# Moving 24 vector blocks of a streaming-trunk kernel from matmul bursts to row sums on VectorE

## What is computed

```python
def modulate(h, shift, scale):
    return h * (1 + scale[:, None, :]) + shift[:, None, :]
...
def sq_relu_mlp(h, w1, w2):
    return jnp.square(jax.nn.relu(h @ w1)) @ w2
```

## Time and profile before

| what | value |
|---|---|
| timed runs (us) | 3221.82, 3226.70, 3227.95; median 3226.7 |
| span of the profiled execution (us) | 3222.3 |
| time of the profiled execution beside its span | not given; span is 4.4 us (0.14%) under the runs' median |
| TensorE matmuls busy | 3134.8 us, 97% of the span |
| VectorE busy | 2185.9 us, 68% |
| ScalarE busy | 1409.6 us, 44% |
| GpSimd busy | 129.3 us, 4% |
| chain that ended last | TensorE 90%, DMA 3%, VectorE 3%, ScalarE 1% |
| moved by DMA | 669.48 MB, 208 GB/s on average |

### The profile page before, as it was taken

How to read it: one execution, slowest core, us unless ns; L and a number is a source line. 1 busy time by engine, 2 the same in 40 slices (tenths; PEclk the granted TensorE clock), 3 DMA queues, 4 the chain that set the end, 5 groups by cost and what they waited for, 6 DMA issues and landing times.

```text
span 3222.3 us, 80509 instructions
## 1 busy us (share of the span) xinstructions
PE 3134.8 (97%) x31624; PEld 2952.1 (92%) x31624; DVE 2185.9 (68%) x3943; ACT 1409.6 (44%) x2323; POOL 129.3 (4%) x245
## 2 busy tenths in 40 slices
PE   7999999998999999999999999999999999999998
PEld 3798888787999999999999988998999999999998
DVE  3676677776578978788788865455589954445445
ACT  2433436665354443333344654334464543343442
POOL 0000001110000000000000000000000000000000
PEclk9999999999999999999999999999999999999999
DMA  9887750002878888888777532432557754444443
GB/s 395 330 292 264 284 206 20 25 24 101 332 288 290 305 299 301 313 298 309 265 240 253 183 119 93 144 124 92 175 191 240 243 170 166 165 163 163 163 164 120
DMA packets 183225, 669.48 MB, mean 208 GB/s; under 512 B 21398, under 2 KB 21568, under 8 KB 182496
## 3 DMA queue, kind: packets, MB, share of 16 engines
q1 hardware_dynamic: 156096, 570.95, 49.3%
q0 software_dynamic: 26912, 95.47, 9.0%
HBM read 662.25 MB, written 4.09 MB: 207 GB/s over the span
## 4 chain that ended last, share of the span: by engine, by line
PE 90%; DMA 3%; DVE 3%; issue 1%; ACT 1%; SPq 1%; DVEq 0%; ACTq 0%; POOLq 0%
PE ps L2281 51%; PE ps L2264 8%; PE ps L2266 7%; PE ps L2265 7%; PE ps L2450 5%; DMA sb_raw<-stream 3%; PE ps L2226 1%; PE ps L2442 1%; PE ps L2215 1%; PE ps L2780 1%; PE ps L2781 1%; PE ps L2782 1%; PE ps L2824 1%; PE ps L2823 1%; PE ps L2394 1%
## 5 line engine op out<-in xcount | busy, mean ns | idle before, releaser
L764 ACT ACTIVATE sb_whi<-sb_raw 128x1024 fp32r<-128x1024 f32 x778 | 812.5, 1058 | 1124.8 <-PE ps L2281 703.8
L1252 DVE TENSOR_TENSOR sb_wlo<-sb_raw,sb_whi 128x1024 fp32r<-128x1024 f32 x778 | 942.7, 1223 | 410.8 <-ACT sb_whi L764 407.7
L2281 PE MATMUL ps<-sb_ah,sb_whi 128*128 128x288 f32 (+1 forms) x2776 | 487.0, 297 | 11.9 <-DVE sb_al L1601 8.2
L2281 PE MATMUL ps<-sb_al,sb_whi 128*128 128x288 f32 (+1 forms) x2776 | 484.4, 297 | 0.0
L2281 PE MATMUL ps<-sb_ah,sb_wlo 128*128 128x288 f32 (+1 forms) x2776 | 482.6, 296 | 0.0
L2281 PEld LDWEIGHTS ps<-sb_ah,sb_whi 128*128 128x128 f32 x2776 | 409.9, 189 | 16.9 <-issue 12.1
L2281 PEld LDWEIGHTS ps<-sb_al,sb_whi 128*128 128x128 f32 x2776 | 409.1, 189 | 0.0
L2281 PEld LDWEIGHTS ps<-sb_ah,sb_wlo 128*128 128x128 f32 x2776 | 408.6, 189 | 0.0
L2264 PE MATMUL ps<-sb_ah,sb_whi 128*128 128x288 f32 (+1 forms) x952 | 286.6, 301 | 2.0 <-DVE sb_x L1451 1.0
L2266 PE MATMUL ps<-sb_al,sb_whi 128*128 128x288 f32 (+1 forms) x952 | 283.1, 297 | 0.0
L2265 PE MATMUL ps<-sb_ah,sb_wlo 128*128 128x288 f32 (+1 forms) x952 | 282.5, 297 | 0.0
(11 more groups left out here) (350 smaller groups left out, 4665.0 us busy)
## 6 DMA issues: line engine op xcount, KB each, us to landing
sb_raw<-stream SPq DMA_DIRECT2D x1070, 512.0 KB, 4.6
sb_strip<-strips POOLq DMA_DIRECT2D x156, 512.0 KB, 5.3
sb_crow<-crow POOLq DMA_DIRECT2D x8, 512.0 KB, 5.9
sb_x<-xT SPq DMA_DIRECT2D x1, 2304.0 KB, 15.5
sb_x<-xT POOLq DMA_DIRECT2D x1, 2304.0 KB, 11.9
yT<-sb_x SPq DMA_DIRECT2D x4, 576.0 KB, 2.8
sb_lwa<-lw POOLq DMA_DIRECT2D x16, 130.0 KB, 2.5
sb_lwg<-lw POOLq DMA_DIRECT2D x16, 130.0 KB, 2.4
```

The source lines that it names most:

```text
L764: nc.scalar.activation(whi[:, q % SPL, :], raw[:, n, :], ACT.Copy).then_inc(hi_ready, 1)
L1252: nc.vector.tensor_tensor(wlo[:, q % SPL, :], raw[:, n, :], whi[:, q % SPL, :], ALU.subtract).then_inc(lo_ready, 1)
L2281: ins = mm(PS[:, m, 0:s.wide], w[:, n % SPL, a:a + P], z[:, 2 * p + j, 0:s.wide], start=False, stop=False)
```

## The change: what it does

The bursts end with m1_0_1: `HALF_GROUPS` goes from 23 to 11. The 12 bursts that go are those of m2_0_1, m1_0_2 and m2_0_2 (four each), with 48 slots of the stream, the copies to `arow` and the finishes. The strips beside m1_0 and m2_0 stay the same in number and now sum blocks 12 x 2 = 24 earlier in the list of vectors; the 24 blocks that come last before the final gate (8 of the shift and all 16 of the scale of `N_MLP1`) become *late rows*.

A late row is 32 outputs: 256 KB of weights in a layout of 128 partitions x 512 (`by_32`), loaded by GpSimd's queue into one of two buffers `late_w`, and two scalar_tensor_tensor instructions of 128x512 with an accumulator on VectorE (`late_rows`). There are 96. GpSimd issues the next load into a buffer when both instructions on it have run. GpSimd's loop over them stands ahead of the four `crow` loads and the late strips, so these now queue behind it, and the late strips also wait for all late rows.

Where the rows run on VectorE: in each of the six `beside` rounds 8 (one before `maxima`, two between `maxima` and `normalise`, one after the split behind it, two after out_lo(0), two after out_lo(1)); in each of the two closings 8 (four after the splits 4 to 7 and before out_lo(0), two after out_lo(0), two after out_lo(1)); in wo0's groups 1 to 3 and in wo1's group 1 8 each, spread by `STRIP_PLACES`. `join_late` (16 copies, 4 additions) turns the sums into `mod` at the start of wo1's group 3, ahead of `gains`.

Two loads of silu's input (`late_c`), two sigmoids on ScalarE at wdq's last slot and two multiplications on VectorE behind wdq make silu(c) in the rows' layout. `osm` and `lroot` get other places in memory, and counts that other waits use move by what was added.

```diff
-        st.append(Stage(f"m1_0_{c}", 4, 8, mixed=c < 3, epi="relu2", src="A"))
-        st.append(Stage(f"m2_0_{c}", 4, 8, mixed=c < 3, epi="resid", src="B", gate=5))
+        st.append(Stage(f"m1_0_{c}", 4, 8, mixed=c < 2, epi="relu2", src="A"))
+        st.append(Stage(f"m2_0_{c}", 4, 8, mixed=c < 1, epi="resid", src="B", gate=5))
...
-HALF_GROUPS = 6 * 4 - 1
+HALF_GROUPS = 3 * 4 - 1
...
+LATE_ROW_BLOCKS = 24
+LATE_ROWS = 4 * LATE_ROW_BLOCKS
+LATE0 = LATE_ROWS0 + LATE_ROW_BLOCKS
+ATT_ROWS, WO_ROWS, HALF_ROWS = 8, 24, 56
...
+            pool.wait_ge(silu_ready, 9)
+            for k in range(2):
+                pool.dma_start(late_w[k][:], d["late"][k]).then_inc(strip_in[k], 16)
+            with pool.Fori(1, LATE_ROWS // 2) as i:
+                for k in range(2):
+                    pool.wait_ge(strip_used, i * 4 + (LATE_USED + 2 * k - 2))
+                    pool.dma_start(late_w[k][:], d["late"][bass.ds(i * 2 + k, 1)].rearrange("a p c -> (a p) c")
+                                   ).then_inc(strip_in[k], 16)
             for i in range(4):
...
+            pool.wait_ge(strip_used, LATE_USED + 2 * LATE_ROWS)
             for k in range(2):
                 pool.dma_start(strip[:, k, :], d["strips"][STRIPS + k]).then_inc(strip_in[k], 16)
...
+                if p == 7:
+                    act.wait_ge(x_back, 128)
+                    for z in range(2):
+                        nc.scalar.activation(late_w[z][:], late_c[z][:], ACT.Sigmoid).then_inc(c_sig, 1)
...
+            def late_rows(first, n, dump, it=0, per=0):
+
+                for i in range(first, first + n):
+                    dve.wait_ge(strip_in[i % 2], it * 8 * per + 16 * (STRIPS // 2 + i // 2 + 1))
+                    if not isinstance(it, int) or i:
+                        dve.wait_ge(strip_used, it * 2 * per + (LATE_USED + 2 * i - 1))
+                    for z in range(2):
+                        nc.vector.scalar_tensor_tensor(
+                            out=late_w[i % 2][:] if z else dump, in0=late_w[i % 2][:], scalar=1.0, in1=late_c[z][:],
+                            op0=ALU.mult, op1=ALU.mult,
+                            accum_out=flat(late_sums[:, bass.ds(it * per + i, 1), z:z + 1])).then_inc(strip_used, 1)
...
+            def join_late():
+
+                dve.wait_ge(strip_used, LATE_USED + 2 * LATE_ROWS)
...
+                    if name == "wo0":
+                        late_rows(WO_ROWS + sum(STRIP_PLACES[:i]), STRIP_PLACES[i], late_scratch, it, 8)
+                    if name == "wo1" and it == 1:
+                        late_rows(HALF_ROWS + WO_ROWS + 8 + sum(STRIP_PLACES[:i]), STRIP_PLACES[i], late_dump)
...
+                            if name == "wo1":
+                                join_late()
                             gains(UNSCALED[name])
...
+            dve.wait_ge(c_sig, 9)
+            for z in range(2):
+                nc.vector.tensor_tensor(late_c[z][:], late_c[z][:], late_w[z][:], ALU.mult).then_inc(silu_ready, 1)
...
-            def outputs(it, v1, v4):
+            def outputs(it, v1, v4, rows=0):
...
                 for h in range(3):
                     out_lo(h).then_inc(S["al_done"], 1)
+                    if h < 2:
+                        late_rows(rows + 2 * h, 2, late_scratch)
...
+                rows = g0 // 4 * HALF_ROWS + it * ATT_ROWS
                 for j in (2, 3):
                     split(s, first + j)
+                late_rows(rows, 1, late_scratch)
                 maxima(v1)
+                late_rows(rows + 1, 2, late_scratch)
                 normalise(v1)
                 split(s, first + 4)
-                outputs(it, v1, v4)
+                late_rows(rows + 3, 1, late_scratch)
+                outputs(it, v1, v4, rows + 4)
...
                     for j in (4, 5, 6, 7):
                         split(s, j)
-                    outputs(3, g0 + 4, 4 * g0 + 12)
+                    late_rows(rows, 4, late_scratch)
+                    outputs(3, g0 + 4, 4 * g0 + 12, rows + 4)
```

More of the change, by code:

```diff
@@ L168 @@
 VECTORS = BY["r"].n0 // RAW
[L169 to L170 removed]
+PLAIN = BY["m2_0_1"].n0
+ADA_SLOTS = PLAIN - BY["m2_0_1"].q0
 HALVED = BY["m1_0_0"].ada0 + 1
[L173 removed]
+HALF_GROUPS = 3 * 4 - 1
 STRIP_GROUPS = 8 * 4 - 1
@@ L399, in trunk @@
         pt = att("pt", [P, 2, 384])
-        osm = att("osm", [P, P])
+        osm = work[:, 6, 0:P]
         trig = sb("trig", [P, 2, T], "MIDS")
@@ L2171, in lead @@
                 def lead():
+                    rows = g0 // 4 * HALF_ROWS + WO_ROWS
                     for j in (2, 3):
@@ L3026 @@
     first, cut = vectors(later[:, :512]), P * (STRIP0 - HALF0) + 512
-    bursts = by_burst(later[:, 512:cut])
+    bursts, late = by_burst(later[:, 512:cut]), P * (LATE_ROWS0 - 6 * KB)
     parts = [own[:64].reshape(2, 4, 8, P, HS).transpose(1, 0, 2, 3, 4).reshape(64, P, HS)]
@@ L3089 @@
         "crk": np.stack([np.repeat(a[n][0].reshape(4, 1, ROW), 32, 1).reshape(P, ROW) for n in ("c_prompt", "c_sample")]),
-        "crow": np.stack([a["c_prompt"][0], a["c_sample"][0]]), "strips": strips(later[:, cut:]),
+        "crow": np.stack([a["c_prompt"][0], a["c_sample"][0]]), "strips": strips(np.concatenate([later[:, cut:late], later[:, late + P * LATE_ROW_BLOCKS:]], 1)),
+        "late": by_32(later[:, late:late + P * LATE_ROW_BLOCKS]),
         "con": constants(), "vec": vec, "lw": lw, "s0": s0,
```

62 lines of the change are left out of this document (43 added, 19 removed).

## The result

The changed kernel took 3238.87 us in the median (3233.8 to 3242.95, 4 runs) against 3225.38 before (3221.82 to 3227.95, 4 runs, one more than the three listed ahead of the prediction): a ratio of 1.0044, 95% interval 1.0031 to 1.0058. A later repeat gave 1.0034 (1.0022 to 1.0047). So the change costs 0.3 to 0.4%, some 11 to 14 us. The forecast, 3231.1 us and "no change", had the wide range (3217 to 3246) and the sign of the difference right, but the time lies beyond the 0.2% that it called no change, and above its own range of 3221 to 3233.

The account below looks back on a forecast made before the run. TensorE, its matmuls filling 97% of the span, was taken as the bound. Costs 22.6 + 5.5 + 2.4 + 1.0 + 0.3 = 31.8 less gain 27.4 gave 4.4 us more: 3231.1 us, range 3217 to 3246.

Parts of the forecast that it names:

- The gain: Twelve bursts removed from TensorE, four at 2.10 us and eight at 2.37: 27.4 us gained.
- The closings: In wo0 and wo1, rows ahead of the last out_lo stall TensorE 8.8 us each, clock 2.5 more: 22.6 us both.
- the forecast's own formula: In a closing, TensorE's stall is 3L - 1.7 in all: 8.8 us for L = 3.5.
- L: Time until a late row's buffer is full again, release through landing: 3.5 us, bounds 3.1 and 4.4 or 4.5.
- A row's work: On VectorE, two instructions of 0.66 us make 1.3 us a late row, 125 us for 96.
- The attention rounds: Six rounds, each 0.4 us longer from late maxima after 0.6 absorbed: 2.4 us; the first attention stage's start 0.3.
- The join: At wo1's last group, join delays the epilogue and next group's first matmul: 4.0 us plus 1.5 for the clock, 5.5.
- The other groups: wo0's groups 1 to 3 and wo1's group 1: four turns of each buffer fit; 1.0 us for all, 0 to 3.
- the forecast's own signs of being wrong: Closings under 7 or over 12 us, attention rounds over 1 us longer, full clock after stalls, TensorE waiting in unnamed places.
- The likeliest case: Whole kernel: 4.4 us slower net, 3231.1 us, called no change; own range 3221 to 3233, chance 0.43.
- the first rival: Rows' loads come slower beside the stream, L = 4.4: costs 44.6 less 27.4, +17.2, 3243.9 us; chance 0.38.
- 12 L - 10.2: The summed costs of the change in terms of L; they reach 27.4 + 6.45 from L = 3.7 on.

Follow-up runs that it names:

- 16 blocks: Against the changed kernel: 16 blocks as late rows instead of 24, four bursts back, rows re-placed, none in wo1, join earlier; 0.9936 to the kernel before, 3199.25 us, unaltered again 0.9956.
- the join alone: The smaller form with 64 late rows, none in wo1, but join_late() back at the start of wo1's fourth group; 0.9960 to the kernel before.

## Why the prediction came out as it did

**The gain**: right. 27.4 us by group periods, 27.7 in the profile.

**The closings**: right in mechanism and nearly in size, 22.6 us forecast, 24.4 measured. The three turns and the two waits were found where they were said to be, at 3.9 and 4.8 us instead of 2.7 and 6.1. That they come to 8.70 us where 8.8 were forecast is in part luck, for two errors cancel. The first turn was slower: 5.2 us from release to row (the load issued at 2012.26 was awaited until 2016.81), while the later two took the 3.5 us of the forecast (issue at 2018.77, row at 2021.62, with 0.7 from release to issue ahead of it). The reason given for 3.5, that the stream moves little in the closings, did not hold in that turn: from 2012 to 2017 us the stream's queue moved 0.52 MB, as much as the two rows' loads, and from 2017 to 2024 us none. By the forecast's own formula the two waits would then have been 10.5 us. But TensorE had less left to wait for at slot 6, since it ran its slot 5 partly at the low clock: without its idle time, the stretch from sample_back to slot 6 took 5.70 us instead of 4.05, 1.65 us longer. The clock took 12.2 - 8.7 = 3.5 us a closing instead of 2.5: these 1.65 between the waits, where they only shorten the second one, and 1.6 in slot 6 behind it.

**L**: right for a quiet queue, with 2.8 us from issue to landing at best and 3.1 in the median over all 96 rows, so L is 3.5 to 3.8. An estimate from the Trainium skill's figures ("DMA: Bandwidth & Descriptors", Anatomy of one DMA) is 2.6 us for a load of this size; that is near the fastest loads (2.8 us here, 2.6 in the repeat) and not the median (3.1 and 3.2). What the forecast left out is that L is not one number: with the stream at work beside them, loads of the closing and of wo1 took 4.5 to 5.1 us from issue to row, so L was 5.2 and more.

**A row's work**: right. The first two rows of the closing start 1.22 us apart (2010.31 and 2011.53), where 1.3 was taken from the earlier trace rows. The half throughput that the Trainium skill ("Vector Engine (DVE) Microarchitecture Reference", section 7) states for this form with two sources in SBUF that are not bf16 would have shown as about twice that, unless the price of the earlier trace rows had it already; the instructions took 0.69 us each, against 0.72 in the kernel before, so a price of twice that is out. Nor is a halving seen beside another instruction: a row sum of 128x1024 (L1407) took 1.22 us, as long as a split, a tensor_tensor of the same size with two fp32 sources.

**The attention rounds**: 2.4 us forecast and 0.3 for the start, 0.3 + 0.8 measured. The estimate that 0.6 us would be absorbed was too cautious: with 16 blocks and the same eight rows a round, the two stretches took 0.1 us more than before the change and nothing.

**The join**: 5.5 forecast. Measured alone, 3.4; in the changed kernel the two groups grew by 2.2 + 4.0 = 6.2. The place was in part wrong: the join delayed a split in the group, and the forecast's wait of some 4 us for the epilogue was 0.25 with the join alone. The difference, 2.8 us, came with the late rows of wo1 and the loads queued behind them: without these rows the two groups took 56.7 us, with the rows but without their loads 56.2, with the join alone 56.0, in the changed kernel 58.7. So it was the loads and not the rows' work; whether the rows' or those behind them was not separated.

**The other groups: this is the step that failed.** The forecast gave wo0's groups and wo1's second group 1.0 us together, 3 at most, since four buffer turns of L + 1.3 fit a group of 25 us. They took 3.2 + 5.1 = 8.3 us, so 7.3 more, which is the whole of the 7.3 us by which the stage sum missed (11.7 against 4.4); the errors of the other terms cancel. One of the forecast's own signs of being wrong, TensorE waiting in the groups of wo0, came true. The step averaged over the group. The rows do not stand evenly: the last places of `STRIP_PLACES` hold two rows just ahead of the epilogue, and a row that waits there holds up the epilogue itself; and in wo1 the last two rows began 5.1 and 4.7 us after their loads were issued, where 2.8 was taken for a load. The run without loads (25.6 us in the third group) shows for wo1 that it was these waits and not the work; for wo0 no run separates the two. Why the loads were slow there is not shown: the stream and, for the last rows, a crow load moved data beside them.

**The chances.** The likeliest case was off by 7 to 10 us, and the outcome lay between it and the first rival, whose price (17.2 us) came nearer. Its reason holds in part: the median load makes L 3.8, just over the 3.7 from which it was to decide, and by 12 L - 10.2 this gives some 8 us of loss, of the 11.7. But its own sum was not what came: it had 28.0 us for the closings (24.4 measured), 7.8 for attention (1.1) and 3.0 for the groups (8.3). The loads were slow in a few places, and in the groups they stood ahead of the one instruction that TensorE waits for. So the mechanism of the closings was foreseen, and that the time lies in the wide range owes as much to its width, whose upper end is the rival's price.

## What to carry to other kernels

In this kernel, work moved from the full engine to one with idle time was free only where three things held at its very place: the idle time was there, its data could land there with the buffers at hand, and nothing that the full engine waits for stood close behind it in program order. Look for these three elsewhere too. With two buffers, count turns (release, issue, landing), not instructions: two rows already loaded cost nothing in the closing, eight cost 12 us. When a change loses a little, look for the part that gives and the part that takes: here two thirds of the blocks, at chosen places, keep their share of the gain whole, and with the last third, and the join where it stood, more was lost than all of them gave.
